# Token blocks with a side-by-side high and low tail in a three-branch encoder layer

## The chip, the cores and the metric

The kernel runs on one core of a Trainium2 chip. The metric is the device time of one execution, in microseconds (us); the number quoted is the median of the runs. Engines: PE is TensorE (its weight loads are listed apart, as PEld), DVE is VectorE, ACT is ScalarE, POOL is GpSimd, SP issues most of the DMAs. PSUM has eight banks of 512 fp32 columns, `bank[0]` to `bank[7]` in the code.

## The reference, cut to what matters

The program is a two-layer encoder trunk for 320 tokens (256 prompt tokens and 64 sample tokens) of width 1024. Each layer makes one wide projection of x, feeds three branches (latent attention, mLSTM, gMLP), merges them, and ends with a mixture of experts. Two parts of the projection matter here, the value half of the gMLP and the mLSTM values:

```python
z = x @ w_in[l] + b_in[l]
cq, ckv, kr, mq, mk, mv, mi, mf, mo, gu, gv, gt = _split(z)
...
v = _layernorm(jax.nn.gelu(v), ln_g, ln_b)          # gMLP: v is gv, (tokens, 512)
sp = jnp.einsum('gts,bcsgd->bctgd', w, vc) + bs...  # mixes over the tokens
...
C_new = decay[..., None, None] * C + jnp.einsum('bhs,bhse,bhsd->bhed', ws, v, k)   # mLSTM: v is mv
```

Both contract over tokens afterwards, so these columns are wanted with the tokens on the partitions.

## The kernel before, in words

All fp32 products are made from fp16 pairs. x is split into `xhi` and `xlo` (the rest), each weight block of 128 x 1024 into `whi` (made by ScalarE, L549) and `wlo` (made by VectorE, L1042), and a product is the sum of three passes: hi by hi, lo by hi, hi by lo. Weight blocks are numbered; SP loads them eight deep, four converted blocks are held (`slot`), and the signals `hi_done`, `lo_done` and `blk_done` pass each block from ScalarE to VectorE to TensorE and back.

There is no planner. Each engine has its own instruction stream, written out by hand, and the order below is the order of that text. The engines meet only at semaphores, each `Signal` with a value per layer.

- Most blocks are z blocks (`z_block`, `group`, L1732): a 128-column tile of the weights is stationary and all 320 tokens stream past, 24 matmuls a block. The result has channels on the partitions.
- Eight blocks a layer are token blocks (`tok_block`, L1748 to L1758): here a tile of tokens is stationary and 128 weight columns stream. `TILES` (L102) cuts the tokens into 128, 128 and 64, so the third token tile, the sample tokens, is a stationary tile of only 64 columns. Each tile takes 8 input chunks by 3 passes, 24 matmuls, into its own 128 columns of one bank: 72 matmuls a block.
- The front of a layer has z blocks 0 to 4 (gates and latents), and then token blocks 5 to 8, the four column tiles of gv. Behind block 5 TensorE makes the sums of squares for the RMS norms (L1841), which wait for ScalarE's squares `sq_c` (L629, L632).
- Then come four mLSTM heads of eight blocks each; the third block of a head is its token block, the values. Behind it stand the transposes of k (L1875) and the key-query products (L1878). In head 0 L1875 also waits for `cols_sb`, small columns that VectorE copies (L1257 to L1260) after its whole work on gv.
- `tok_out` (L1195 to L1201, VectorE) takes a token block out of its bank: one instruction for the two full tiles (L1197), one for the third (L1200, partitions 0 to 63); each multiplies by the scale `UN` and adds the bias `row`. It signals `tokv`. In the front ScalarE then applies Gelu (L681, L683), after which VectorE makes the statistics of the layer norm (L1232, L1235). In a head VectorE goes on to the weighted values `v_ws` (L1274, L1275) and to `att` (L1280, L1282), and TensorE uses `v_ws` at L1888, after one z block.
- At the start of a layer ScalarE loads a function table (L594), waits for `x_split` (all of `xlo` is made), in layer 0 issues six loads from its queue (L603), copies the layer's parameters (L605 to L608), and then converts weight blocks and evicts z blocks in turn (L615). In layer 0 it waits for those six loads at L625.

Of the kernel before, what the change touches and what calls it, by code (L numbers as in the profile page):

```python
# [33 lines left out]
F32, F16 = mybir.dt.float32, mybir.dt.float16  # L34
ALU = mybir.AluOpType
ACT = mybir.ActivationFunctionType
# [3 lines left out]
P = 128  # L40
DM, L = 1024, 2
TP, TS, PAST = 256, 64, 256
T = TP + TS
KD = DM // P
# [18 lines left out]
UN = 1.0 / (WS * XS)  # L63
# [38 lines left out]
TILES = [(0, P), (P, P), (2 * P, TS)]  # L102
# [15 lines left out]
def build_trunk(nc, d):  # L118
    with ExitStack() as ctx:
        def sb(name, shape, dt=F32):  # L120
            return ctx.enter_context(nc.sbuf_tensor(name, shape, dt))

        def sig(name, per, before=0):
            return Signal(ctx, nc, name, per, before)
# [3 lines left out]
        whi = sb("whi", [P, SLOTS, BLK], F16)  # L128
        wlo = sb("wlo", [P, SLOTS, BLK], F16)

        xT = sb("xT", [P, KD * T])
        xhi = sb("xhi", [P, KD, T], F16)
        xlo = sb("xlo", [P, KD, T], F16)
        acc = sb("acc", [P, KD * T])
        ysq = sb("ysq", [P, 4, T])
        br_hi = sb("br_hi", [P, 12 * T], F16)
# [122 lines left out]
        bank = [ctx.enter_context(nc.psum_tensor(f"bank{i}", [P, 512], F32)) for i in range(8)]  # L259
# [71 lines left out]
        m_hi = sig("m_hi", KD)  # L331
        m_lo = sig("m_lo", KD)
        acc_pre = sig("acc_pre", 2)
        y_done = sig("y_done", 2 * KD)
        y_sq = sig("y_sq", 2 * KD)
        y_sum = sig("y_sum", 2)
# [203 lines left out]
        def _(act):  # L540
            A = nc.scalar.activation
# [48 lines left out]
            for l in range(0, L):  # L590
# [2 lines left out]

                act.preload_act_table_set(LN_EXP)  # L594
                act.wait_ge(x_split.sem, x_split.value(l, 0))

                for dst, src in () if l else ((cache, d["cache"][bass.ds(l * P, P), :]),
                                 (kr[:, 0:PAST], d["krope"][bass.ds(l * ROPE, ROPE), :]),
# [436 lines left out]
        def _(dve):  # L1035
            V = nc.vector
# [87 lines left out]
            for l in range(0, L):  # L1124
# [37 lines left out]
                for c in range(NCH):  # L1162
                    s = c if c < 4 else 5
# [31 lines left out]
                def tok_out(b, dst2, dst1, row, last):  # L1195

                    V.scalar_tensor_tensor(dst2, bank[b][:, 0:2 * P].rearrange("p (i n) -> p i n", i=2),  # L1197
                                           UN, row.unsqueeze(1).broadcast_to([P, 2, P]), ALU.mult,
                                           ALU.add)
                    V.scalar_tensor_tensor(dst1, bank[b][0:TS, 2 * P:3 * P], UN, row[0:TS, :],  # L1200
                                           ALU.mult, ALU.add).then_inc(last.sem, 1)  # L1201

                for i in range(4):
# [42 lines left out]
                for h in range(0, MH):  # L1246
# [25 lines left out]
                    for i, (t0, n) in enumerate(TILES):  # L1272
                        w = cols[0:n, bass.ds(h + (3 + i) * MH, 1)]
# [141 lines left out]
                for u in range(UNITS):  # L1415
# [7 lines left out]
                    b = bank[4 + u % 2]  # L1423
                    w = 2 if u % 3 < 2 else 1
# [298 lines left out]
        def _(pe):  # L1723
            M = nc.tensor.matmul
# [23 lines left out]
            def tok_block(l, n, s, b):  # L1748

                ready(l, n)  # L1750
                for i, (t0, m) in enumerate(TILES):
                    j = 0
                    for k in range(KD):
                        for x, w in ((xhi, whi), (xhi, wlo), (xlo, whi)):
                            ins = M(bank[b][0:m, i * P:(i + 1) * P], x[:, k, t0:t0 + m],  # L1755
                                    w[:, s, k * P:(k + 1) * P], start=(j == 0), stop=(j == 3 * KD - 1))
                            j += 1
                ins.then_inc(blk_done.sem, 1)  # L1758

            def unread(b, n):  # L1760
# [40 lines left out]
            for l in range(0, L):  # L1801
# [4 lines left out]
                for g in range(5):  # L1806
# [17 lines left out]
                    for k in range(KD):  # L1824

                        pe.wait_ge(x_split.sem, x_split.value(l, k + 1 - KD))
                        for w, part in ((whi, 0), (whi, 1), (wlo, 0)):
                            a = M(bank[0][:, 0:T], w[:, 0, k * P:(k + 1) * P], x_rhs(part, k),
                                  start=(k == 0 and w is whi and part == 0),
                                  stop=(k == KD - 1 and w is wlo))  # L1830
                    a.then_inc(blk_done.sem, 1)
                for i in range(4):
# [4 lines left out]
                    if i == 0:  # L1837
                        for k in range(2):
                            pe.wait_ge(sq_c.sem, sq_c.value(l, k + 1))
                            for c in range(2):  # L1840
                                a = M(bank[4 + k][:, 0:T], ones_dm[:, :], ysq[:, 2 * k + c, :],  # L1841
                                      start=(c == 0), stop=(c == 1))
# [4 lines left out]
                for h in range(0, MH):  # L1847
# [29 lines left out]
                    for i, (t0, n) in enumerate(TILES):  # L1877
                        a = M(bank[5][0:n, i * P:i * P + n], mk[:, t0:t0 + n], mq[:, t0:t0 + n],  # L1878
                              start=True, stop=True)
# [6 lines left out]
                    for c in range(NCH):  # L1886
                        r0, b, o = CH * (c % 2), bank[6 + c % 2], (c // 2) * (DH + 1)
# [594 lines left out]
```

## Time and profile before

| | us |
|---|---|
| median of 3 runs | 1082.61 |
| lowest, highest | 1082.49, 1086.24 |
| profiled execution, its time | 1087.75 |
| its span, first to last instruction | 1086.0 |
| PE busy | 1023.6 |
| DVE busy | 827.3 |
| ACT busy | 660.3 |
| mean granted TensorE clock | 0.986 of full speed |

The profile is of one execution; its engine times are set against its own span. Matmuls are pipelined, and their recorded durations overlap: what one costs is the distance between the starts of two neighbours, not its duration. The end of a matmul is modelled. An idle time in brackets names what ended it.

### The profile page before, as it was taken

The page shows a single profiled execution, that of the slowest core. Times are in us where ns is not written, and L with a number is a line of the kernel's source. Part 1 is how long each engine was busy: PE and PEld are TensorE (multiplying, and loading weights), DVE is VectorE, ACT ScalarE, POOL GpSimd, SP SyncE. Part 2 cuts the span into 40 slices and gives each one's busy share as a digit, 9 for nine tenths or more (in the row PEclk, how much of TensorE's full clock was granted, in tenths as well). Part 3 has the DMA queues.
Part 4 walks back from the last instruction along what each step waited for, and adds up shares of the span by engine and source line. Part 5 has one row for each costly group of instructions (what it writes and reads, how often), then busy time and mean ns, then how long its engine had stood idle before and what let it go on. Part 6 is the DMA issues. An engine that isn't in the chain of part 4 may idle for free. (4 is left out here: it accounts for less than half of the span.)

```text
span 1086.0 us, 24604 instructions
## 1 busy us (share of the span) xinstructions
PE 1023.6 (94%) x10126; PEld 786.3 (72%) x10126; DVE 827.3 (76%) x1484; ACT 660.3 (61%) x1059; POOL 0.7 (0%) x10
## 2 busy tenths in 40 slices
PE   6999999999998799999999999999999978999995
PEld 4877777777776699965567777777777658999443
DVE  4786677654898699989887766676559877999886
ACT  5565455754365777767767445556534676777764
POOL 0000000000000000000000000000000000000000
PEclk9999999999999899999999999999999998999998
DMA  9754444323462389988735534443244415999861
GB/s 348 268 167 143 140 142 129 108 98 116 156 235 78 114 299 327 333 281 312 280 118 192 165 122 137 141 139 98 98 136 156 155 45 187 332 324 328 294 260 51
DMA packets 59653, 205.06 MB, mean 189 GB/s; under 512 B 7088, under 2 KB 10348, under 8 KB 59020
## 3 DMA queue, kind: packets, MB, share of 16 engines
q1 hardware_dynamic: 55980, 195.96, 53.2%
q10 hardware_dynamic: 3552, 7.42, 1.9%
q8 instruction: 84, 1.38, 0.5%
q14 instruction: 37, 0.30, 0.1%
HBM read 198.77 MB, written 3.40 MB: 186 GB/s over the span
## 5 line engine op out<-in xcount | busy, mean ns | idle before, releaser
L1042 DVE SCALAR_TENSOR_TENSOR wlo<-w,whi 128x1024 f16<-128x1024 f32 x358 | 429.7, 1220 | 76.9 <-ACT whi L549 75.3
L549 ACT ACTIVATE whi<-w 128x1024 f16<-128x1024 f32 x358 | 370.6, 1049 | 93.6 <-PE bank L1732 52.2
L1732 PE MATMUL bank<-xhi,whi 128*128 128x320 f16 x704 | 211.0, 300 | 0.0
L1732 PE MATMUL bank<-xhi,wlo 128*128 128x320 f16 x704 | 210.5, 299 | 0.0
L1732 PE MATMUL bank<-xlo,whi 128*128 128x320 f16 x704 | 210.5, 299 | 0.0
L1732 PE MATMUL bank<-arena_b,whi 128*128 128x128 f16 x2048 | 183.4, 222 | 0.0
L1732 PE MATMUL bank<-arena_b,wlo 128*128 128x128 f16 x1024 | 179.2, 222 | 0.0
L1732 PEld LDWEIGHTS bank<-arena_b,whi 128*128 128x128 f16 x2048 | 160.0, 99 | 0.0
L1732 PEld LDWEIGHTS bank<-arena_b,wlo 128*128 128x128 f16 x1024 | 101.6, 99 | 0.0
L1732 PEld LDWEIGHTS bank<-xhi,whi 128*128 128x128 f16 x704 | 68.8, 98 | 30.3 <-issue 2.5
L1732 PEld LDWEIGHTS bank<-xhi,wlo 128*128 128x128 f16 x704 | 68.9, 98 | 26.8
L1732 PEld LDWEIGHTS bank<-xlo,whi 128*128 128x128 f16 x704 | 68.9, 98 | 26.1 <-issue 1.4
L1755 PE MATMUL bank<-whi,xhi 128*128 128x128 f16 (+1 forms) x384 | 66.4, 220 | 0.0
L1755 PE MATMUL bank<-wlo,xhi 128*128 128x128 f16 (+1 forms) x384 | 66.0, 219 | 0.0
L1755 PE MATMUL bank<-whi,xlo 128*128 128x128 f16 (+1 forms) x384 | 66.0, 219 | 0.0
L1732 PE MATMUL bank<-br_hi,whi 128*128 128x320 f16 x192 | 57.4, 299 | 0.0
L1732 PE MATMUL bank<-br_lo,whi 128*128 128x320 f16 x192 | 57.4, 299 | 0.0
L1732 PE MATMUL bank<-br_hi,wlo 128*128 128x320 f16 x192 | 57.4, 299 | 0.0
L2253 PE MATMUL bank<-whi,arena_a 128*128 128x512 f16 x128 | 48.6, 379 | 1.8 <-DVE wlo L1042 1.8
L2253 PE MATMUL bank<-wlo,arena_a 128*128 128x512 f16 x128 | 48.5, 379 | 0.0
L2253 PE MATMUL bank<-whi,arena_b 128*128 128x512 f16 x128 | 48.5, 379 | 0.0
L694 ACT ACTIVATE arena_a<-bank,par_h 128x320 f32<-128x320 f32 x24 | 12.7, 527 | 58.6 <-PE bank L1732 58.6
(357 smaller groups left out, 1751.6 us busy)
## 6 DMA issues: line engine op xcount, KB each, us to landing
w<-in_w SPq DMA_DIRECT2D x358, 512.0 KB, 4.7
arena_b<-head_rows ACTq DMA_DIRECT2D x2, 1920.0 KB, 7.2
xT<-in_x SPq DMA_DIRECT2D x2, 640.0 KB, 4.9
out_y<-xT SPq DMA_DIRECT2D x4, 320.0 KB
rows<-in_rows ACTq DMA_DIRECT2D x1, 1024.0 KB, 11.3
rows<-in_rows SPq DMA_DIRECT2D x1, 1024.0 KB, 5.8
out_ckv<-arena_a SPq DMA_DIRECT2D x2, 320.0 KB
acc<-kr SPq DMA_DIRECT2D x2, 288.0 KB
```

The costliest lines, as they stand in the source:

```text
L549: A(whi[:, n % SLOTS, :], w32[:, n % RAW, :], ACT.Copy, scale=WS).then_inc(hi_done.sem, 1)
L694: A(dst, bank[(M0 + step) % 4][:, 0:T], func, scale=scale, bias=par_t[:, bass.ds(col, 1)]).then_inc(z_ev.sem, 1)
L1042: V.scalar_tensor_tensor(wlo[:, n % SLOTS, :], w32[:, n % RAW, :], WS, whi[:, n % SLOTS, :], ALU.mult, ALU.subtract).then_inc(lo_done.sem, 1)
L1732: ins = M(out, w[:, s, sub * P:(sub + 1) * P], rhs(part, k), start=(n == 0), stop=(n == 3 * len(subs) - 1))
L1755: ins = M(bank[b][0:m, i * P:(i + 1) * P], x[:, k, t0:t0 + m], w[:, s, k * P:(k + 1) * P], start=(j == 0), stop=(j == 3 * KD - 1))
L2253: a = M(b[:, :], h_[:, bass.ds(g * (8 * CAP) + ((2 * q + kt) * CAP + H0), CAP)], w[:, slot(l, n), kt * 512:(kt + 1) * 512], start=(q == 0 ...
```

## The change

ScalarE builds a new tile `x_tail` at the start of each layer with two copies: for each of the 8 input chunks the 64 sample-token columns of `xhi` and, beside them, the 64 of `xlo`, 128 columns together. In a token block the two full tiles stay as they are. For the third, each input chunk has one matmul with `x_tail` stationary and `whi` streaming, which puts hi by hi on partitions 0 to 63 and lo by hi on partitions 64 to 127 of the same bank columns, and one with the 64-column `xhi` tile stationary and `wlo` streaming, added on partitions 0 to 63. The latter comes one chunk behind the former. `tok_out` takes the third tile out in two instructions with a drain between: partitions 64 to 127 times the scale plus the bias, and then partitions 0 to 63 times the scale plus that result. TensorE waits for the new signal `tail_set` at the start of each token block.

```diff
@@ -131,6 +131,7 @@
         xT = sb("xT", [P, KD * T])
         xhi = sb("xhi", [P, KD, T], F16)
         xlo = sb("xlo", [P, KD, T], F16)
+        x_tail = sb("x_tail", [P, KD, 2 * TS], F16)
         acc = sb("acc", [P, KD * T])
         ysq = sb("ysq", [P, 4, T])
         br_hi = sb("br_hi", [P, 12 * T], F16)
@@ -331,6 +332,7 @@
         m_hi = sig("m_hi", KD)
         m_lo = sig("m_lo", KD)
         acc_pre = sig("acc_pre", 2)
+        tail_set = sig("tail_set", 1)
         y_done = sig("y_done", 2 * KD)
         y_sq = sig("y_sq", 2 * KD)
         y_sum = sig("y_sum", 2)
@@ -593,6 +595,8 @@
 
                 act.preload_act_table_set(LN_EXP)
                 act.wait_ge(x_split.sem, x_split.value(l, 0))
+                A(x_tail[:, :, 0:TS], xhi[:, :, TP:T], ACT.Copy)
+                A(x_tail[:, :, TS:P], xlo[:, :, TP:T], ACT.Copy).then_inc(tail_set.sem, 1)
 
                 for dst, src in () if l else ((cache, d["cache"][bass.ds(l * P, P), :]),
                                  (kr[:, 0:PAST], d["krope"][bass.ds(l * ROPE, ROPE), :]),
@@ -1197,7 +1201,10 @@
                     V.scalar_tensor_tensor(dst2, bank[b][:, 0:2 * P].rearrange("p (i n) -> p i n", i=2),
                                            UN, row.unsqueeze(1).broadcast_to([P, 2, P]), ALU.mult,
                                            ALU.add)
-                    V.scalar_tensor_tensor(dst1, bank[b][0:TS, 2 * P:3 * P], UN, row[0:TS, :],
+                    V.scalar_tensor_tensor(dst1, bank[b][TS:P, 2 * P:3 * P], UN, row[TS:P, :],
+                                           ALU.mult, ALU.add)
+                    dve.drain()
+                    V.scalar_tensor_tensor(dst1, bank[b][0:TS, 2 * P:3 * P], UN, dst1,
                                            ALU.mult, ALU.add).then_inc(last.sem, 1)
 
                 for i in range(4):
@@ -1748,13 +1755,23 @@
             def tok_block(l, n, s, b):
 
                 ready(l, n)
-                for i, (t0, m) in enumerate(TILES):
+                pe.wait_ge(tail_set.sem, tail_set.value(l, 1))
+                for i, (t0, m) in enumerate(TILES[0:2]):
                     j = 0
                     for k in range(KD):
                         for x, w in ((xhi, whi), (xhi, wlo), (xlo, whi)):
-                            ins = M(bank[b][0:m, i * P:(i + 1) * P], x[:, k, t0:t0 + m],
-                                    w[:, s, k * P:(k + 1) * P], start=(j == 0), stop=(j == 3 * KD - 1))
+                            M(bank[b][0:m, i * P:(i + 1) * P], x[:, k, t0:t0 + m],
+                              w[:, s, k * P:(k + 1) * P], start=(j == 0), stop=(j == 3 * KD - 1))
                             j += 1
+                for k in range(KD):
+                    if k:
+                        M(bank[b][0:TS, 2 * P:3 * P], xhi[:, k - 1, TP:T], wlo[:, s, (k - 1) * P:k * P],
+                          start=False, stop=False)
+                    if k == KD - 1:
+                        M(bank[b][0:TS, 2 * P:3 * P], xhi[:, k, TP:T], wlo[:, s, k * P:(k + 1) * P],
+                          start=False, stop=False)
+                    ins = M(bank[b][:, 2 * P:3 * P], x_tail[:, k, :], whi[:, s, k * P:(k + 1) * P],
+                            start=(k == 0), stop=(k == KD - 1))
                 ins.then_inc(blk_done.sem, 1)
 
             def unread(b, n):
```

## Rows read from the trace of the kernel before

**Rows 1.** The page: busy time by engine, and the chain that ended last by line.

```profile
PE 1023.6 (94%) x10126; PEld 786.3 (72%) x10126; DVE 827.3 (76%) x1484; ACT 660.3 (61%) x1059; POOL 0.7 (0%) x10
...
PE bank L1732 20%; DVE wlo L1042 3%; PE bank L2253 3%; PE bank L2095 2%; ACT whi L549 1%; PE bank L1755 1%; PE bank L2170 1%; DVEq L1653 1%; PE bank L2269 1%; PE bank L1950 1%; PE bank L2080 1%; DVE xT L1055 1%; PE bank L1984 1%; PE bank L2180 0%; PE bank L2026 0%
```

**Rows 2.** Windows, heads of layer 1: stretch, length, busy (instructions), clock, DMA share, GB/s.

```profile
595.00:725.00 130.00, 129.54 (x1086) 98.86 (x1087) 93.59 (x206) 67.82 (x107) 0.00 (x0) 1.00 0.46 144
```

**Rows 3.** Timeline of PE, its waits: start, us, engine, line, form, [idle before].

```profile
33.95 0.54 PE L1841 MATMUL bank<-ysq,ones_dm 128*128 128x320 f32 x1 [1.08 <-ACT ysq L629]
...
61.96 0.30 PE L1875 MATMUL bank<-ident,mk 128*128 128x128 f32 x1 [0.65 <-DVE cols L1260]
...
595.46 0.30 PE L1875 MATMUL bank<-ident,mk 128*128 128x128 f32 x1 [2.43 <-DVE cols L1260]
```

**Rows 4.** Timeline of PE, one token block: its start, then the third tile's.

```profile
28.57 0.22 PE L1755 MATMUL bank<-whi,xhi 128*128 128x128 f16 x1
...
31.19 0.22 PE L1755 MATMUL bank<-whi,xlo 128*128 128x128 f16 x1
31.34 0.24 PE L1755 MATMUL bank<-whi,xhi 128*64 128x128 f16 x1
31.42 0.22 PE L1755 MATMUL bank<-wlo,xhi 128*64 128x128 f16 x1
```

**Rows 5.** Timeline of the weight loads (PEld) at the same place.

```profile
31.14 0.10 PEld L1755 LDWEIGHTS bank<-whi,xlo 128*128 128x128 f16 x1
31.34 0.11 PEld L1755 LDWEIGHTS bank<-whi,xhi 128*64 128x64 f16 x1
31.37 0.11 PEld L1755 LDWEIGHTS bank<-wlo,xhi 128*64 128x64 f16 x1
```

**Rows 6.** Timeline of PE, layer 1: second token block's start, then the third's.

```profile
568.97 0.22 PE L1755 MATMUL bank<-whi,xhi 128*128 128x128 f16 x1
...
573.05 0.22 PE L1755 MATMUL bank<-whi,xlo 128*64 128x128 f16 x1
573.21 0.23 PE L1755 MATMUL bank<-whi,xhi 128*128 128x128 f16 x1
573.27 0.22 PE L1755 MATMUL bank<-wlo,xhi 128*128 128x128 f16 x1
```

**Rows 7.** Timeline of PE, from a z block to a token block.

```profile
562.35 0.30 PE L1732 MATMUL bank<-xhi,wlo 128*128 128x320 f16 x1
562.48 0.22 PE L1755 MATMUL bank<-whi,xhi 128*128 128x128 f16 x1
```

**Rows 8.** Timeline of ACT in the front of layer 1.

```profile
573.37 1.06 ACT L549 ACTIVATE whi<-w 128x1024 f16<-128x1024 f32 x1 [4.53 <-PE bank L1755]
...
583.70 0.42 ACT L681 ACTIVATE arena_b<-arena_b 128x256 f32<-128x256 f32 x1 [0.91 <-DVE arena_b L1200]
```

**Rows 9.** Timeline of DVE: neighbours with a drain between, and without.

```profile
568.61 0.32 DVE L1174 TENSOR_SCALAR arena_a<-arena_a 4x320 f32<-4x320 f32 x1
569.00 0.41 DVE L1180 TENSOR_TENSOR arena_a<-arena_a,m_at 4x256 f32<-4x256 f32 x1
...
583.06 0.42 DVE L1197 SCALAR_TENSOR_TENSOR arena_b<-bank,rows 128x256 f32<-128x256 f32 x1
583.39 0.27 DVE L1200 SCALAR_TENSOR_TENSOR arena_b<-bank,rows 64x128 f32<-64x128 f32 x1
```

**Rows 10.** Timeline of DVE in head 1 of layer 1.

```profile
628.05 0.42 DVE L1197 SCALAR_TENSOR_TENSOR arena_c<-bank,rows 128x256 f32<-128x256 f32 x1 [1.41 <-PE bank L1755]
...
633.46 0.23 DVE L1294 COPY c_st<-c_init 128x129 f32<-128x129 f32 x1 [2.19 <-PE bank L1888]
```

**Rows 11.** Timeline of ACT at the start of both layers.

```profile
15.81 0.27 ACT L605 ACTIVATE par_c<-par 128x82 f32<-128x82 f32 x1 [1.28 <-issue]
...
31.28 0.63 ACT L625 ACTIVATE kv_hi<-c_st 128x512 f16<-128x512 f32 x1 [5.10 <-DMA c_init<-in_c_init]
...
566.88 1.06 ACT L549 ACTIVATE whi<-w 128x1024 f16<-128x1024 f32 x1 [1.90 <-PE bank L1755]
```

## The prediction

> **What bounds the kernel now.** I read the busy shares and the chain first. TensorE is busy 94% of the span and the longest entry of the chain is one of its matmul lines, so the time it needs is mostly the time the kernel takes [rows 1]. The stretch in which the four mLSTM heads of layer 1 run says it more sharply (layer 0's is like it): of 130 us TensorE is busy 129.54, VectorE 93.59, ScalarE 67.82, at a granted clock of 1.00 (the 2.4 GHz level) [rows 2]. There a nanosecond of TensorE is a nanosecond of the end. It is not so in the front of a layer (20 to 62 us and 555 to 596 us): there TensorE waits 1.08 us for ScalarE's squares in layer 0 (L1841), and at the door of head 0 (L1875) for VectorE's `cols`, 0.65 us in layer 0 and 2.43 us in layer 1 [rows 3]. Sixteen token blocks are touched: four in each front, one in each head.
>
> How one block runs now decides the forecast. Its 48 matmuls on 128-column tiles start from 28.57 to 31.19, 47 steps in 2.62 us or 0.0558 us a step [rows 4]; on 64-column tiles the step is the same. So far the change looks like 8 matmuls saved. But the rows show something between the second and the third token tile. The last matmul on a 128-column tile starts at 31.19, the first on a 64-column tile at 31.34, and the next at 31.42: two steps take 0.23 us in place of 0.112 [rows 4]. The weight loads say why: normally a load starts one step ahead of its matmul, beside the matmul before; at the change of shape it starts at 31.34, together with its matmul, 0.20 us after the load before it (31.14), and the next follows at 31.37 [rows 5]. The way back from 64 to 128 columns costs the same: 573.05, 573.21, 573.27, two steps in 0.22 us [rows 6]. A change of instruction group without a change of shape costs nothing: after a z block TensorE goes from 562.35 to 562.48, the usual pace for 320 columns, though a wait on a semaphore stands there [rows 7]. So a change of the stationary shape costs 0.118 one way and 0.108 the other, 0.113 us on average. Check: 72 x 0.0558 + 2 x 0.113 = 4.24 us, and the second token block begins at 568.97, the third at 573.21, 4.24 us later [rows 6].
>
> **TensorE, part by part.** The first two token tiles keep their 48 matmuls. The third had 24 matmuls on a 64-column tile. It gets 8 on the 128-column `x_tail` (T) and 8 on the 64-column `xhi` tail (h), in the order T h T h T h T h T h T h T h h T. That order is the whole case: it changes shape at every step but one, 14 times, where the old one changed twice (in and out). The entry from tile two to the first T and the exit from the last T are free now. New block: 64 x 0.0558 + 14 x 0.113 = 3.57 + 1.58 = 5.15 us, against 4.24: +0.91 us a block. The saved 8 matmuls bring 0.45 us, the 12 further changes take 1.36 us. The trace has no place where the f16 shape changes at every step, so the price is bounded. From below: nothing, if loads can go ahead when the changes follow each other. From above: each matmul must end as modelled (0.22) and then the load run (0.11) [rows 4, 5], a step of 0.33 and a block of about 7.4 us. I take 0.113, the nearest rows, in both directions. If the late start of the first matmul after a change doesn't add up, it is 0.095 (0.15 less 0.056), and the block costs +0.68.
>
> The Trainium skill, TensorEngine Tiling (Array Packing), section Key Properties, says that changing the tiling mode drains TensorE. By this rule, the trace agrees that a change costs, and it speaks against this change. TensorE: Matmul & The Clock Gate of the Trainium skill, Step-by-step, gives the drain that normally overlaps as about 128 cycles; an estimate from it is 0.053 us a change, and the sum would be +0.19 us a block. The rows at a change say twice that, and I go by them.
>
> **The way of the +0.91 to the end.**
> Heads 1 to 3 of both layers, six blocks: TensorE is never idle, so all of it counts: 6 x 0.91 = 5.5 us.
> Front of layer 0: the first block's +0.91 hides in the 1.08 us wait for ScalarE [rows 3]. Three more and that of head 0 make 4 x 0.91 = 3.64; 0.65 of it replaces the wait at L1875, since VectorE's chain there moves by less (below). That leaves +3.0 us.
> Front of layer 1: five blocks, 4.55 us, less the 2.43 us of wait: +2.1. Here VectorE's chain must be followed too. ScalarE's weight conversion at 573.37 waits for the second token block (4.53 us idle, released by it) [rows 8], so it moves 2 x 0.91 = 1.8 us. What follows on ScalarE to the Gelu of the third tile at 583.70, which waits for VectorE, moves along, and so do the normalised latents, the batch statistics and `cols`. The third tile's additional sum adds 0.35. So `cols` come 1.8 + 0.35 = 2.2 us later: both paths give +2.1 to +2.2. I take +2.1.
> Sum: 5.5 + 3.0 + 2.1 = +10.6 us.
>
> **VectorE.** Each block's third tile is now two instructions of 0.27 us with a drain between. An instruction follows its forerunner 0.33 us after the start without a drain (583.06 to 583.39), and 0.07 us after its end with one (568.61 + 0.32 to 569.00) [rows 9]. So 0.27 + 0.07 = 0.35 us a block, 16 times 5.6 us in all. In the heads it hides: VectorE waits 1.41 us for the block to end and after this work 2.19 us for L1888 [rows 10]; the four instructions of `v_ws` stand behind it, then `att`, and TensorE needs them only after a z block of 3.3 us. If that cover went, it would cost 0.35 us a head, 2.8 us. In the fronts it is in the chain above: 0 in layer 0 (TensorE is last), up to 0.35 in layer 1. Bounds for the fronts are 0 and 8 x 0.35.
>
> **ScalarE's two copies into `x_tail`.** The nearest row is a conversion of 512 elements a partition, 0.63 us [rows 11]; two make 1.1 to 1.2 us a layer; bounds 0.3 (a parameter copy, `par_c`, takes 0.27 [rows 11]) and twice 0.63, 1.3. In layer 0 ScalarE sits idle 1.28 us before `par_c`, while the six loads that its queue issues go out [rows 11]; the copies fit there. What they are queued ahead of are those six DMAs; if the queue lets them wait for the copies, the last load, for which ScalarE waits at 31.28, comes up to 1.2 us later, and that is on the path. I take 0. In layer 1 the copies delay `par_c`, the fifth block's conversion and the first evictions by 1.2; TensorE has blocks three and four to run meanwhile, whose weights are ready or come in time, and ScalarE's next real wait, 1.90 us at 566.88 [rows 11], takes it up. TensorE's new wait on `tail_set` comes two z blocks after the copies and finds it set; if it didn't, all of TensorE would stand behind it. The reuse in layer 1 is safe in ScalarE's own order.
>
> **Sum and baseline.** The profiled execution took 1087.75 us (span 1086.0), 5.1 us above the median of the runs, 1082.61; the additions don't depend on which. 1087.75 + 10.6 = 1098.3 for such an execution, and 1082.6 + 10.6 = **1093.2 us** for the median. A hundredth of a microsecond in the price of a change moves 14 x 0.01 = 0.14 us a block, some 2 us in all.
>
> **Rivals.**
> *Free changes (not slower).* The loads of alternating shapes go ahead of the running matmuls, and only 64 steps are left: 3.57 us a block, -0.67. Place: the 16 steps of the third tile; it decides the sign where a change costs under (4.24 - 3.57)/14 = 0.048 us. The heads give 6 x 0.67 = 4.0; the fronts, where VectorE then is last, only 0.3 and 1.0. Time 1077.3 us. For it: within a shape every load does go ahead [rows 5]. Against: both directions cost alike, the same in every block that I read. The Trainium skill, TensorE: Matmul & The Clock Gate, Step-by-step, says loads are pulled ahead when they target the background weight buffer; no row at a change shows it. Chance 8%.
> *Half price.* A change costs one skipped step, 0.056 us: 64 x 0.0558 + 14 x 0.056 = 4.36 us, +0.12 a block; heads 0.7, fronts some 1 us by VectorE's sum: 1084.5 us. Against: the rows show the double. Chance 6%. The drain estimate from the Trainium skill's page above (TensorE: Matmul & The Clock Gate, Step-by-step) would come out here.
> *Dear changes.* The step of 0.33 gives +3.2 us a block: heads 19, fronts 5 x 3.2 less the waits, 14 and 13.6: about 1129 us. A price in between, 0.15, gives 14 x 0.037 = 0.5 us more a block, and 1101. Together 11%; against the far end speaks that the load at 31.34 didn't wait for the modelled end (31.41).
>
> **How the numbers follow.** The main case, prices of 0.095 to 0.12 with 0 to 2 us of copies and sums beside it, has 75%: 1090 to 1096. Leaving out the free case, the top of the dear ones and little more, the range is 1086 to 1101. About 0.5% is what a measurement can tell from no change, 1077.2 and 1088.0. Slower by more: 75% + 11%, less 2% for the low tail of the main case, 84%. Within: half price 6%, that tail 2%, part of the free case 3%: 11%. Faster: 5%.
>
> **What would show it.** In the profile after, a token block from its first start to the next group's should take 5.1 us (4.24 before), and in its last 16 matmuls each step 0.15 to 0.175 us; weight loads there should start with their matmuls. The three heads without a wait should each be 0.9 us longer. The waits at L1875 should be near zero in both layers. The new VectorE line should show 16 instructions of 0.27 us, and no new wait at L1888. Steps of 0.056 in the third tile would make the prediction wrong, and so would a wait on `tail_set` or later loads in layer 0.

## The result, and the profile after

The changed kernel takes **1093.51 us** (median of 5 runs, 1091.93 to 1095.31), the kernel before in the same comparison 1082.82: slower, ratio 1.0091 (95% interval 1.0063 to 1.0119), or +10.7 us between the medians. The forecast was +10.6 us and 1093.2.

The page after, its busy row. TensorE has 128 matmuls less than in [rows 1] (16 blocks by 8) and is busy 8.2 us longer.

```profile
PE 1031.8 (95%) x9998; PEld 783.0 (72%) x9998; DVE 833.0 (76%) x1500; ACT 662.9 (61%) x1063; POOL 0.7 (0%) x10
```

The third tile of a token block in the timeline of PE after, to be read against [rows 4]: start, duration, engine, line, operation and shape. L1773 is the 128-column `x_tail`, L1768 and L1771 the 64-column tile.

```profile
31.22 0.22 PE L1763 MATMUL bank<-whi,xlo 128*128 128x128 f16 x1
31.27 0.22 PE L1773 MATMUL bank<-whi,x_tail 128*128 128x128 f16 x1
31.42 0.24 PE L1768 MATMUL bank<-wlo,xhi 128*64 128x128 f16 x1
31.60 0.23 PE L1773 MATMUL bank<-whi,x_tail 128*128 128x128 f16 x1
31.76 0.24 PE L1768 MATMUL bank<-wlo,xhi 128*64 128x128 f16 x1
31.93 0.23 PE L1773 MATMUL bank<-whi,x_tail 128*128 128x128 f16 x1
...
33.44 0.24 PE L1768 MATMUL bank<-wlo,xhi 128*64 128x128 f16 x1
33.52 0.22 PE L1771 MATMUL bank<-wlo,xhi 128*64 128x128 f16 x1
33.67 0.23 PE L1773 MATMUL bank<-whi,x_tail 128*128 128x128 f16 x1
```

The entry into `x_tail` takes a normal step (31.22 to 31.27). From then on every matmul starts 0.15 to 0.18 us after the one before. The one step without a change (33.44 to 33.52) takes 0.08.

The weight loads at the same place, against [rows 5]: each load after a change of shape starts with its matmul and not one step ahead of it.

```profile
31.22 0.10 PEld L1773 LDWEIGHTS bank<-whi,x_tail 128*128 128x128 f16 x1
31.42 0.11 PEld L1768 LDWEIGHTS bank<-wlo,xhi 128*64 128x64 f16 x1
31.59 0.10 PEld L1773 LDWEIGHTS bank<-whi,x_tail 128*128 128x128 f16 x1
31.76 0.11 PEld L1768 LDWEIGHTS bank<-wlo,xhi 128*64 128x64 f16 x1
```

One whole block in the timeline of PE, its first matmul and that of the next block, against [rows 6]: 5.14 us where 4.24 stood.

```profile
37.57 0.22 PE L1763 MATMUL bank<-whi,xhi 128*128 128x128 f16 x1
...
42.65 0.23 PE L1773 MATMUL bank<-whi,x_tail 128*128 128x128 f16 x1
42.71 0.22 PE L1763 MATMUL bank<-whi,xhi 128*128 128x128 f16 x1
```

The two doors of head 0 in the timeline of PE, against [rows 3]. In layer 0 no wait is left (65.09 to 65.16), in layer 1 it is 0.22 us.

```profile
65.09 0.23 PE L1773 MATMUL bank<-whi,x_tail 128*128 128x128 f16 x1
65.16 0.50 PE L1892 MATMUL bank<-ident,mk 128*128 128x128 f32 x3
...
599.23 0.52 PE L1892 MATMUL bank<-ident,mk 128*128 128x128 f32 x3 [0.22 <-DVE cols L1267]
```

The heads of layer 1 as a window, against [rows 2] (length, busy and instructions by engine, granted clock): TensorE is now busy all of the time at clock 1.00.

```profile
600.00:725.00 125.00, 125.00 (x1005) 93.19 (x1005) 89.06 (x196) 60.90 (x94) 0.00 (x0) 1.00 0.45 138
```

I cut both traces at the same instructions. A front ends at the transposes of head 0; it is counted from the start of the span in layer 0 and from its first matmul in layer 1. The heads go from these transposes to the first values of the latent attention (L1950 before, L1967 after), 125.5 us before in both layers. After less before, front and heads: +3.2 and +2.6 us in layer 0, +2.3 and +2.6 in layer 1, together 10.7. (The first matmul of layer 0 starts at 10.56 us before and 10.26 after; counted from there the front would be +3.5. Its first token block starts at 28.57 and 28.59.) The layer 0 figure is not exact to the tenth: e10 below has the same code up to its door of layer 0, and its front was 1.0 us shorter than that of the kernel before (its door at 60.96 against 61.96), by an earlier end of ScalarE's squares.

The two profiled executions themselves lie only 5.1 us apart (1092.83 and 1087.75). The rest stands outside the touched stages: the mean granted clock was 0.986 in the one before and 0.992 in the one after, because the one before has more stretches at the 1.2 GHz level.

Over the runs of one kernel the time goes with that mean, by about 1.0 us for each 0.001 (27 runs of the kernel before, 1079.0 to 1086.8 us). Where I say "at equal clock" below, the means over the runs are corrected by that slope; it is my own correction, and a rough one. Within the 12 runs of another kernel the slope is anything from 0.1 (e5) to 1.2 us (e3), and the correction also takes out what a low clock behind a longer wait has cost. The after kernel comes to +10.5 at equal clock.

### The profile page after: what moved, and what is told of

The parts are those of the page before. It is cut to its first block and busy times, and to the rows that moved or that the text cites. A ratio compares the mean times of both kernels' runs of the same rounds, so it can differ in the third digit from the quotient of the medians.

```text
span 1091.0 us, 24392 instructions
## 1 busy us (share of the span) xinstructions
PE 1031.8 (95%) x9998; PEld 783.0 (72%) x9998; DVE 833.0 (76%) x1500; ACT 662.9 (61%) x1063; POOL 0.7 (0%) x10
## 5 line engine op out<-in xcount | busy, mean ns | idle before, releaser
L1739 PE MATMUL bank<-arena_b,whi 128*128 128x128 f16 x2048 | 181.0, 220 | 0.0
L1739 PE MATMUL bank<-arena_b,wlo 128*128 128x128 f16 x1024 | 176.8, 220 | 0.0
L1763 PE MATMUL bank<-whi,xhi 128*128 128x128 f16 x256 | 43.7, 219 | 0.0
L1763 PE MATMUL bank<-wlo,xhi 128*128 128x128 f16 x256 | 43.7, 219 | 0.0
L1763 PE MATMUL bank<-whi,xlo 128*128 128x128 f16 x256 | 43.7, 219 | 0.0
```

The source lines that it names most:

```text
L1739: ins = M(out, w[:, s, sub * P:(sub + 1) * P], rhs(part, k), start=(n == 0), stop=(n == 3 * len(subs) - 1))
L1763: M(bank[b][0:m, i * P:(i + 1) * P], x[:, k, t0:t0 + m], w[:, s, k * P:(k + 1) * P], start=(j == 0), stop=(j == 3 * KD - 1))
```

## The experiments

Eleven kernels ran, each in five rounds against the kernel before. The question behind them: is the price the change of shape (my theory), and if it is, where does the saving of 8 matmuls a block go once the price is gone? The times expected below start from 1082.6 us. Beside e1 to e4 the kernel before had a median of 1084.08 us, beside e5 to e8 1083.97, and beside e9 to e11 1083.11.

**e1, the same 16 matmuls, two changes in place of 14.** `x_tail` first, the narrow ones together, the last wide one at the end (`wide` is a matmul with `x_tail` stationary, `narrow` one with the 64-column tile):

```diff
...
+                for k in range(KD - 1):
+                    wide(k)
+                for k in range(KD):
+                    narrow(k)
+                ins = wide(KD - 1)
```

> The changed kernel with the third tile's 16 matmuls in another order: seven on x_tail, the eight 64-column ones together, the last on x_tail. 2 changes of shape in a block in place of 14, the same instructions. Theory (a change of the stationary shape costs 0.113 us): block 64 x 0.0558 + 2 x 0.113 = 3.80 us (4.24 before, 5.14 changed kernel), three heads 1.3 us faster than before each layer, fronts ended by VectorE's chain and within 0.5 us of before; about 1080 us. Rival (what is slow is the narrow accumulation onto partitions 0 to 63 of columns that were just written, whatever the order): as the changed kernel, 1093 us.

Measured: 1084.55 us, ratio 1.0005 (0.9987 to 1.0022). Of the loss of 10.7 us nearly all is gone, with the same instructions in another order, which shows the price to be the changes. The third tile in the timeline of PE:

```profile
31.54 0.55 PE L1767 MATMUL bank<-whi,x_tail 128*128 128x128 f16 x7
32.02 0.63 PE L1771 MATMUL bank<-wlo,xhi 128*64 128x128 f16 x8
32.59 0.23 PE L1767 MATMUL bank<-whi,x_tail 128*128 128x128 f16 x1
```

First and last stand 1.05 us apart: 15 steps of 0.0558 and 0.21 for two changes. But the 3 us of gain expected are not there in the times (at equal clock they are, -2.8). The timeline of PE at the doors, and the windows behind the door of layer 1:

```profile
63.30 0.87 PE L1896 MATMUL bank<-ident,mk 128*128 128x128 f32 x3 [3.34 <-DVE cols L1267]
...
594.34 0.87 PE L1896 MATMUL bank<-ident,mk 128*128 128x128 f32 x3 [4.94 <-DVE cols L1267]
```

```profile
592.00:596.00 4.00, 1.66 (x8) 1.43 (x8) 3.90 (x9) 3.75 (x6) 0.00 (x0) 0.50 0.50 153
596.00:600.00 4.00, 4.00 (x22) 2.53 (x22) 3.08 (x12) 1.86 (x5) 0.00 (x0) 0.66 0.70 247
600.00:604.00 4.00, 4.00 (x34) 2.85 (x33) 1.92 (x8) 1.47 (x2) 0.00 (x0) 1.00 0.80 207
```

The faster blocks end earlier, the wait for VectorE's `cols` grows to 3.3 and 4.9 us, and after it TensorE runs at 0.50, the 1.2 GHz level: 22 matmuls in a window that holds 34 at the full clock.

**e2, no change of shape at all.** Both `whi` and `wlo` stream past `x_tail`, which also adds lo by lo:

```diff
+                for k in range(KD):
+                    for w in (whi, wlo):
+                        ins = M(bank[b][:, 2 * P:3 * P], x_tail[:, k, :], w[:, s, k * P:(k + 1) * P],
+                                start=(k == 0 and w is whi), stop=(k == KD - 1 and w is wlo))
```

> The changed kernel with x_tail stationary in all 16 matmuls of the third tile, streaming whi and then wlo for each chunk (adds the low by low product). No change of shape. Theory: block 64 x 0.0558 = 3.57 us, 0.67 less than before; heads 6 x 0.67 = 4.0 us faster, fronts 0.3 and 1.0 faster: 1077.5 us, the free case of the prediction. Rival (16 alternating weights or the loads of x_tail cost something themselves): steps over 0.06 us in the third tile and more than 1080 us.

Measured: 1081.78 us, ratio 0.9979 (0.9960 to 0.9999). The blocks are what was expected: the third tile of a block in head 1 starts at 128.01 and its sixteenth matmul at 128.85, 15 steps of 0.056. The time is 4.3 us above the expectation, of which 1.5 is the slower kernel before of this comparison. The door in the timeline of PE, and two windows from it:

```profile
592.68 0.87 PE L1887 MATMUL bank<-ident,mk 128*128 128x128 f32 x3 [5.96 <-DVE cols L1267]
```

```profile
590.00:594.00 4.00, 1.32 (x7) 1.32 (x7) 3.90 (x9) 3.75 (x6) 0.00 (x0) 0.59 0.53 141
594.00:598.00 4.00, 4.00 (x18) 2.33 (x18) 3.42 (x13) 2.20 (x6) 0.00 (x0) 0.55 0.74 252
```

In the kernel before, behind its wait of 2.43 us [rows 3]:

```profile
598.00:602.00 4.00, 4.00 (x35) 2.85 (x33) 2.98 (x11) 2.77 (x5) 0.00 (x0) 1.00 0.59 193
```

So the saved matmuls of the front turn into idle time before a door that VectorE holds, and the clock then falls: the heads, which should have shrunk from 125.5 to 123.5 us, took 126.3 and 125.7.

**e3, eight changes.** Two wide, two narrow, in turn:

```diff
...
+                for k in range(0, KD - 2, 2):
+                    wide(k)
+                    wide(k + 1)
+                    narrow(k)
+                    narrow(k + 1)
+                wide(KD - 2)
+                narrow(KD - 2)
+                narrow(KD - 1)
+                ins = wide(KD - 1)
```

> The changed kernel with the third tile in pairs, T T h h T T h h ..., 8 changes of shape a block. Theory, if every change costs alike: block 3.57 + 8 x 0.113 = 4.48 us, +0.24 on before, heads +1.4 us, fronts about +1: 1085.5 us. Rival (only changes that follow each other directly add up, or the hidden late start is paid once a run of changes): steps after a pair of equal shapes shorter, block under 4.3 us and 1083 us.

Measured: 1087.84 us, ratio 1.0039 (1.0017 to 1.0061); +3.7 at equal clock. A pair takes 0.22 to 0.23 us, two steps and one change of about 0.11. With 2, 8 and 14 changes the times stand in the order that a price per change gives. e3 is 2.3 us above my number; 1.5 of that is the slower kernel before of this comparison. The profile also shows a clock of 0.79 behind the door of layer 1 (after 2.23 us of wait).

**e4, VectorE's part alone.** The kernel before, with the third tile's instruction made twice and a drain between:

```diff
                     V.scalar_tensor_tensor(dst1, bank[b][0:TS, 2 * P:3 * P], UN, row[0:TS, :],
+                                           ALU.mult, ALU.add)
+                    dve.drain()
+                    V.scalar_tensor_tensor(dst1, bank[b][0:TS, 2 * P:3 * P], UN, row[0:TS, :],
                                            ALU.mult, ALU.add).then_inc(last.sem, 1)
```

> The kernel before with VectorE's part alone: the third tile is taken out twice, with the drain between (the same value is written twice). Theory: hidden in the heads (0), and in the chain of both fronts once, +0.4 us a layer: 1083.5 us. Rival (VectorE binds the heads too): +0.35 to 0.48 us a head, 8 times, and 1087 us.

Measured: 1086.62 us, ratio 1.0030 (1.0011 to 1.0048), +1.9 at equal clock. The time is nearer to the rival's 1087 than to my 1083.5, but what the rival says isn't there: the heads are unchanged (125.5 and 125.5). The fronts are +0.1 and +0.3 (+0.3 both, counted from their first matmuls). So it hides in the heads, and costs in a front about one block's worth, since only the last block's instruction stands in the chain. The rest of the time, over 1 us at equal clock and some 2 by the medians, stands in no stage of this profile, and I leave it open. The size of the addition is another point. The timeline of VectorE in e4, and in the changed kernel:

```profile
583.60 0.42 DVE L1197 SCALAR_TENSOR_TENSOR arena_b<-bank,rows 128x256 f32<-128x256 f32 x1
583.93 0.27 DVE L1200 SCALAR_TENSOR_TENSOR arena_b<-bank,rows 64x128 f32<-64x128 f32 x1
584.28 0.28 DVE L1203 SCALAR_TENSOR_TENSOR arena_b<-bank,rows 64x128 f32<-64x128 f32 x1
584.49 0.41 DVE L1197 SCALAR_TENSOR_TENSOR arena_b<-bank,rows 128x256 f32<-128x256 f32 x1
```

```profile
586.34 0.42 DVE L1201 SCALAR_TENSOR_TENSOR arena_b<-bank,rows 128x256 f32<-128x256 f32 x1
586.77 0.29 DVE L1204 SCALAR_TENSOR_TENSOR arena_b<-bank,rows 64x128 f32<-64x128 f32 x1
587.14 0.28 DVE L1207 SCALAR_TENSOR_TENSOR arena_b<-bank,arena_b 64x128 f32<-64x128 f32 x1
587.35 0.41 DVE L1201 SCALAR_TENSOR_TENSOR arena_b<-bank,rows 128x256 f32<-128x256 f32 x1
```

The period of a block on VectorE is 0.89 us in e4 and 1.01 in the changed kernel. In the kernel before it is 0.53 (583.06 to 583.59). The drain and the second instruction give 0.36. A further 0.12 comes with L1204, which reads partitions 64 to 127 and writes 0 to 63: it starts 0.43 behind its forerunner, where an instruction on partitions 0 to 63 starts 0.33 behind, and is 0.02 longer. L1204 starts just when its forerunner ends (586.34 + 0.42). L1200 in e4 starts 0.09 before its forerunner ends (583.60 + 0.42).

**e6, ScalarE's copies and the wait alone.** The kernel before with the two copies and with TensorE's wait on `tail_set`, nothing read from `x_tail`:

```diff
+                A(x_tail[:, :, 0:TS], xhi[:, :, TP:T], ACT.Copy)
+                A(x_tail[:, :, TS:P], xlo[:, :, TP:T], ACT.Copy).then_inc(tail_set.sem, 1)
...
+                pe.wait_ge(tail_set.sem, tail_set.value(l, 1))
```

> The kernel before with ScalarE's two copies into x_tail and TensorE's wait for them; matmuls and eviction as before. Theory: hidden, 0 us (within 0.1%). Rival (they delay the first loads or evictions): up to 1.2 us in each layer, +0.1 to 0.2%, seen in the front of a layer.

Measured: 1082.66 us, ratio 0.9994 (0.9974 to 1.0014). Nothing, as forecast. The fronts are as long as before. But the heads of layer 1 took 127.2 us in this profile, though the wait at their door is the 2.43 us of the kernel before, to the hundredth. The door in the timeline of PE and the window around it:

```profile
590.72 0.52 PE L1880 MATMUL bank<-ident,mk 128*128 128x128 f32 x3 [2.43 <-DVE cols L1264]
```

```profile
590.00:594.00 4.00, 3.28 (x18) 2.21 (x19) 3.90 (x17) 3.74 (x8) 0.00 (x0) 0.74 0.77 266
```

Here the clock fell, in the kernel before it stayed at 1.00 behind the same wait [rows 2]. So one profiled execution doesn't tell what a wait of this length costs in another. In the timeline of ScalarE the copies stand among the loads that its queue issues:

```profile
14.73 0.63 ACT L598 ACTIVATE x_tail<-xhi 128x512 f16<-128x512 f16 x1
14.85 0.57 ACTq L607 DMA_DIRECT2D c_init<-in_c_init  x1
15.27 0.61 ACT L599 ACTIVATE x_tail<-xlo 128x512 f16<-128x512 f16 x1
```

The last load is issued while the first copy runs, and does not wait for the second.

**e7, the cheap block in the heads only.** The fronts keep the old block and the old `tok_out`; the heads have e2's:

```diff
-                    tok_block(l, g, slot(l, g), g % 4)
+                    tok_front(l, g, slot(l, g), g % 4)
...
-                    tok_out((5 + i) % 4, gvt...
+                    front_tok_out((5 + i) % 4, gvt...
```

> The token blocks and the eviction of the front as in the kernel before; in the heads the third tile as in e2_all_tail. Theory: TensorE reaches the door of head 0 0.67 us earlier than before, waits there 1.3 and 3.1 us, VectorE's chain is not lengthened, and the six head blocks gain 4.0 us: 1079 us by the clock of before; the wait of 3.1 us may draw the half clock in layer 1 in some runs. Rival (VectorE's second instruction binds the heads): heads gain less than 1 us a layer.

Measured: 1081.03 us, ratio 0.9986 (0.9970 to 1.0003). Layer 0 does as expected: wait 1.2 us, heads 123.4. In layer 1 the wait is 3.0 us (2.43 before, plus the one cheap block of head 0 that stands ahead of the door), the clock falls to 0.60 in the window 594 to 598, and the heads take 125.1. The interval of the ratio holds 1, so the times alone show no gain.

**e8, e2 with work put into the wait.** 24 matmuls of 320 columns whose results nobody reads, ahead of the transposes of head 0:

```diff
                     tok_block(*zb(2, 5, 3))
+                    if h == 0:
+                        unread(6, 24)
```

> e2_all_tail with 24 matmuls of 320 columns into an unused bank (their result is not read) where TensorE waits at head 0 of each layer for VectorE's cols; 24 x 0.136 = 3.3 us, less than the waits of 4.2 and 6.0 us seen there. Theory (the freed TensorE time turned into a longer idle wait, after which the granted clock fell to the 1.2 GHz level for 6.8 us in both layers): no half-clock stretch at 60 to 67 and 589 to 596 us, the heads 125.5 - 2.0 = 123.5 us in both layers, 2 x 2.6 us less than in e2_all_tail: about 1078 us. Rival (the clock stretch has another cause): the heads stay at 126 us and the time at 1082 or above.

Measured: 1079.98 us, ratio 0.9962 (0.9948 to 0.9977). The windows at both doors, to be read against e2's above:

```profile
60.00:64.00 4.00, 2.99 (x24) 2.09 (x21) 3.90 (x10) 3.76 (x6) 0.00 (x0) 1.00 0.40 130
64.00:68.00 4.00, 4.00 (x33) 2.83 (x34) 3.82 (x13) 2.82 (x8) 0.00 (x0) 1.00 0.83 253
590.00:594.00 4.00, 2.03 (x17) 1.64 (x17) 3.89 (x10) 3.74 (x7) 0.00 (x0) 1.00 0.61 167
594.00:598.00 4.00, 4.00 (x34) 2.85 (x33) 3.17 (x14) 2.83 (x6) 0.00 (x0) 1.00 0.70 238
```

The clock stays at 1.00 and the heads take 123.4 us in both layers: 2.1 us less than before, where the rival *free changes* has three blocks by 0.67 us. More work for TensorE made the heads 2.9 and 2.3 us shorter than in e2. Over the runs only 1.8 us of that show between e2 and e8; 0.7 us went into a longer front of layer 0 (its door at 63.09 against 62.41), the rest I cannot place. The runs bear the clock out: its mean over the 12 runs is 0.987 in e2 and 0.990 in e8, and likewise 0.987 in e5 and 0.991 in e11 below.

**e5, no `x_tail`: two 64-column tiles side by side.** 24 matmuls as before, but they write partitions 0 to 63 and 64 to 127 in turn; VectorE adds the halves as in the change:

```diff
+                for k in range(0, KD, 2):
+                    for kk, r, x, w in ((k, 0, xhi, whi), (k, TS, xlo, whi), (k, 0, xhi, wlo),
+                                        (k + 1, TS, xhi, wlo), (k + 1, 0, xhi, whi), (k + 1, TS, xlo, whi)):
...
+                        ins = M(bank[b][r:r + TS, 2 * P:3 * P], x[:, kk, TP:T],
+                                w[:, s, kk * P:(kk + 1) * P], start=first[r], stop=last)
```

> No x_tail: the third tile takes 24 matmuls on 64-column tiles, alternating between partitions 0 to 63 and 64 to 127 of the same columns (12 each), then VectorE adds the halves as in the changed kernel; two changes of shape a block as before. Theory A (price is for a change of shape only, and matmuls run one after the other): block 4.24 us as before, and about 1086 us with VectorE's additional work, as e4_dve_only. Theory B (a change of the output half is a change too): 24 steps of 0.168, block 6.7 us, +2.5, and over 1115 us. Theory C (the two halves of the array run side by side): 12 x 0.0558 + 2 x 0.113 = 0.9 us for the tile, block 3.57 us, as e2_all_tail.

Measured: 1081.21 us, ratio 0.9977 (0.9963 to 0.9992). The third tile in the timeline of PE:

```profile
31.60 0.22 PE L1760 MATMUL bank<-whi,xlo 128*128 128x128 f16 x1
31.75 0.24 PE L1768 MATMUL bank<-whi,xhi 128*64 128x128 f16 x1
31.76 0.24 PE L1768 MATMUL bank<-whi,xlo 128*64 128x128 f16 x1
31.83 0.22 PE L1768 MATMUL bank<-wlo,xhi 128*64 128x128 f16 x2
31.89 0.22 PE L1768 MATMUL bank<-whi,xhi 128*64 128x128 f16 x1
31.89 0.22 PE L1768 MATMUL bank<-whi,xlo 128*64 128x128 f16 x1
```

Two matmuls start within 0.01 us, and the pairs follow each other by 0.056: 12 steps for 24 matmuls. The Trainium skill, TensorEngine Tiling (Array Packing), section Key Properties, says that different tiles can load and multiply in parallel; the trace agrees. The doors' waits were 4.35 and 5.13 us, with 1.2 GHz behind them as in e2, so the time is e2's. The output moves from one half of the partitions to the other at every matmul here, and that costs nothing. Where a price was paid, the width of the output changed together with that of the stationary tile; no run parts these two.

**e11, e5 with the same 24 extra matmuls; e9, everything that helped; e10, the control.** e9 has the old blocks in the fronts, e5's block in the heads, and fitted extra work at the doors. e10 is the kernel before with extra work at the door of layer 1 only:

```diff
+                    if h == 0:
+                        unread(6, 24)                    # e11
+                        unread(6, 20 if l else 8)        # e9
+                    if h == 0 and l:
+                        unread(6, 16)                    # e10
```

> e5_halves with 24 extra matmuls of 320 columns (about 3.2 us), whose results nobody reads, at the door of the first head of both layers, where e5_halves waits 4.4 and 5.1 us. Theory (the wait's length sets whether the clock falls after it): clock 1.00 in the stretches after both doors, heads 122.7 each where e5_halves has 125.6 and 125.8, fronts as e5_halves; time 1079.2. Rival (the 0.48 us a block of VectorE holds the door as late as the saved TensorE time was early): heads 123.4 or above, time 1080 as e8_filler.

> The layer fronts as in the kernel before (24 matmuls of the third tile, one VectorE instruction), the blocks of the heads as in e5_halves (64-column tiles in alternating output halves, VectorE adds them), no x_tail and no copies, and 8 (layer 0) and 20 (layer 1) extra matmuls of 320 columns, whose results nobody reads, at the door of the first head. Theory (the front is bound by VectorE and ScalarE, so a cheaper block there only adds idle time before the door; idle time at the door lowers TensorE's clock for what follows): front stages as before (51.4 and 50.4 us, within 0.4), heads 122.7 each (e8_filler's 123.4 less 3 blocks x 4 steps of 0.056), clock 1.00 at both doors; time 1078.5, ratio 0.995. Rival (the halves save nothing here because what precedes the door waits for VectorE, whose second instruction is 0.48 us a block): heads 123.4 or above, time 1080 or above.

> The kernel before with only 16 extra matmuls of 320 columns, whose results nobody reads, at the door of the first head of layer 1, where it waits 2.4 us. Theory (the extra work stands in idle time, and only an idle wait longer than before's costs clock): no change, ratio within 0.999 to 1.001 and time 1082.5. Rival (extra matmuls at the door are worth something by themselves, and e8_filler's gain over e2_all_tail has nothing to do with the longer wait): faster by 1.8 us, as e8_filler stands to e2_all_tail, 1081.

| | us | ratio (95%) | heads, layers 0 and 1 | at equal clock |
|---|---|---|---|---|
| before (of this comparison) | 1083.11 | 1 | 125.5, 125.5 | |
| e10 | 1081.02 | 0.9992 (0.9970 to 1.0015) | 125.5, 125.5 | -0.4 |
| e11 | 1078.06 | 0.9951 (0.9933 to 0.9969) | 123.5, 123.8 | -3.6 |
| e9 | **1076.82** | 0.9958 (0.9938 to 0.9978) | 123.5, 123.5 | -4.8 |

e9 has the lowest median of all and beats both kernels; e11 has the lower ratio, and their intervals overlap, so the two can't be told apart. e10's ratio lies within its expectation, but its median is the rival's 1081, and its interval also holds the rival's 0.9983, so the time doesn't decide. The heads speak for the cheaper blocks as the source of e8's 123.4: with extra work alone they are as long as before (125.5 in both layers). But where the clock would have fallen behind the 2.43 us, as in e6, the extra work may well be worth something by itself; this stays open.

In e9 and e11 I had expected heads of 122.7 us: e5's 12 steps against e2's 16 are 4 by 0.056 us less a block. They took what e8's take. The expectation had left out my own price: entering and leaving the 64-column tiles are two changes of shape. The timeline of PE in e9, entry and exit of one block:

```profile
123.73 0.22 PE L1780 MATMUL bank<-whi,xlo 128*128 128x128 f16 x1
123.88 0.24 PE L1788 MATMUL bank<-whi,xhi 128*64 128x128 f16 x1
...
124.52 0.22 PE L1788 MATMUL bank<-whi,xlo 128*64 128x128 f16 x1
124.67 0.44 PE L1910 MATMUL bank<-ident,mk 128*128 128x128 f32 x2
```

Each step takes 0.15 us where e2's take 0.056, and the step behind the entry is longer too. Four steps saved are 0.22 us, two changes by 0.113 are 0.23. The rival of those two expectations was right in the length of the heads, 123.4 or above, but not in its reason: no wait for VectorE stands in these heads. Its time, 1080 or above, was too high.

## Why the prediction was right, point by point

That the total came out within 0.3 us of the forecast is luck in part: the interval of the ratio leaves 6.8 to 12.9 us for the loss, and one front differs by 1.0 us between executions of the same code. The block and the heads are the firm part.

- *The price of a change.* Read from two places in [rows 4 to 6], 0.113 us on average, it held when the changes follow each other at every step. In the block of the first fence the first `x_tail` and the last stand 2.40 us apart. That is 15 steps; less 15 by 0.0558 it leaves 1.56 us for 14 changes, 0.112 each. The variant 0.095 (a late start that doesn't add up; by the prediction's own numbers +0.66 a block, not +0.68) and the dear 0.15 both fall. e1 shows it by order alone, and e3 lies between. Why a change costs this much no run shows; that its weight load doesn't start ahead is all that the rows tell.
- *The block.* 5.15 us forecast, 5.14 measured.
- *The heads.* 2.7 us forecast a layer (3 by 0.91), 2.6 measured in each; the same instruction of neighbouring heads is 33.37 us apart (616.78 to 650.15), before 32.51 (613.02 to 645.53).
- *The fronts.* +3.0 and +2.1 forecast, +3.2 and +2.3 measured. Both waits at the door were used up, as forecast; in layer 1 0.22 us is left. The first block's +0.91 did go into the wait for ScalarE's squares in layer 0: 0.36 us of the 1.08 is left (L1858), and the squares came 0.3 us later than before.
- *VectorE.* This term was too small: 0.48 us a block against 0.35. Its place was right, hidden in the heads, and only the end of a front feels it: in layer 1 that fits the 0.2 us by which the front came out longer. e4's time lies above what its stages show.
- *ScalarE.* Copies of 0.63 and 0.61 us, in e6 1.15 us from the start of the first to the end of the second, as forecast, and hidden (e6). In the changed kernel the last load was issued in the middle of the first copy and the wait on `tail_set` cost nothing.
- *The drain.* The Trainium skill, TensorEngine Tiling (Array Packing), section Key Properties, says that a change of tiling mode drains TensorE. The trace and the runs agree that a change costs time; that it is a drain they don't show. The estimate of 0.053 us from the Trainium skill, TensorE: Matmul & The Clock Gate, section Step-by-step, is half the measured price.
- *The rival of free changes* was right about what would follow without changes in the heads (3 by 0.67 us) but its 1077.3 us was too low even with no changes: e2 took 1081.8. It took the longer wait at the door as harmless, and it is not: the clock behind it falls. Nor did its fronts get 0.3 and 1.0 us shorter; in e2 they are 0.45 and 0.25 us longer than before.
- *The baseline.* Adding to the median, not to the profiled execution, was right: the stages differ by 10.7, the medians by 10.7, the two profiled executions by 5.1.

## What to carry to other kernels

Count changes of the stationary tile's shape, not only matmuls: at 128 streamed columns one change cost two steps here, so grouping the same 16 instructions by shape was worth 9 us, and padding the small tile to the full shape as much or more. Before you make a stage cheaper, look at the wait that ends it: in a front whose end VectorE holds, saved TensorE time only lengthened TensorE's idle time, and the half clock that followed took back more than the heads had gained. Put the saving where the engine never waits, and read the granted clock of the window behind each wait that grew.

## What the runs showed of the hardware that I had not expected

- A longer wait cost clock. In the profiled executions waits at the door of 3.0 to 6.0 us in e1, e2, e5 and e7 were each followed by matmuls at the 1.2 GHz level, while e8, e9, e10 and e11, with extra matmuls in that place and waits of 0.1 to 2.0 us left, show 1.00 there. Between these it can go either way: e3's 2.23 us in layer 1 was followed by a clock of 0.79 in the window 598 to 606 and e6's 2.43 us by 0.74 in the window 590 to 594, but before's 2.43 us and e4's 2.78 us by 1.00.
- Two 64-column stationary tiles that write different halves of the output partitions run side by side, 24 fp16 matmuls in 12 steps of 0.056 us (e5).
- A VectorE instruction that reads PSUM partitions 64 to 127 and writes SBUF partitions 0 to 63 started 0.10 us later behind its forerunner than one that stays in partitions 0 to 63. It started when its forerunner ended; the other one started 0.09 us before that. Which of the two, the upper half or the move across, makes it so, was not tried.
- The time of one kernel varies over its runs by some 0.7% (before: 1079.0 to 1086.8 us), together with the mean granted clock. What sets the clock elsewhere in a run, outside the stretches named, stays open.
